# Transposing the layer's input on TensorE instead of loading it already transposed

## The chip, the cores and the metric

The kernel runs on one core of a Trainium2 chip. The metric is the device time of one execution in microseconds, the median of several runs. The profile shows one execution of it.

## The reference, cut to what matters

One decoder layer over 1024 tokens with 1024 features each, and 16 meta tokens ahead of them. The part that the change touches is the first product:

```python
h = jnp.concatenate([meta, x], axis=1)      # (1, 16 + 1024, 1024)
proj = h @ w_in                              # q, k, v, o_pre and 8 gate columns
...                                          # mLSTM mixer, @ w_out, layer norm
y = hier_moe(h, ...)                         # 32 experts, top 2, gated MLP
h = layer_norm(ALPHA * h + y, ...)
```

All products are computed in close to full float32: each operand is split into a rounded part and a remainder (`hi` and `lo`), and three matmuls (hi·hi, hi·lo, lo·hi) make one product.

## The kernel before, in words

The contraction of `h @ w_in` runs over the features, so TensorE needs the input with features on the partitions and tokens in the columns. The kernel before gets it so from memory: the host wrapper makes `x_cols`, the tokens reordered into 8 tiles of 128 features (partitions) by 8 chunks by 128 tokens, and `meta_cols`, the same for the meta tokens. It makes `x_rows` too, in the ordinary order, which is read later as the residual.

A tile of 512 KB is loaded by `load_x(n)` (L365) on SP's queue into one of two buffers `xt`. For each half tile ScalarE writes the rounded part `xhi` (`x_hi`, L670) and VectorE the remainder `xlo` (`x_lo`, L1011), both straight from `xt`. The weight comes in pieces of 512 columns. Of the first piece four quarters are loaded one by one (L370); ScalarE rounds them in eight steps of 512 elements (`hi_first`, L657) and VectorE subtracts in eight steps (`lo_first`, L999). Later pieces go in halves of 2048 elements (L648, L994).

TensorE does units in order. The first 8 (`o_unit(0)` to `o_unit(7)`) multiply token tile n by the first piece: 8 chunks of 3 matmuls, 24 matmuls of 128x512 (`mm3`, L1645 to L1647). Ahead of unit 0 it runs 14 dummy float32 matmuls on the identity (`awake`, L1723), after unit 7 the gate columns (`gate_rows`, L1680, L1682), then the units of the other pieces, then eight chunks of the mLSTM recurrence mixed with value and output products, the router, and the loop over the experts. Each engine does its list in the order in which it is written; what an engine waits for is a semaphore count that another engine's instruction raises (`x_hi`, `x_lo`, `hi_done`, `lo_done`).

`unit_cp` counts the evacuations of units by ScalarE (`evac`, L683). PSUM has eight banks; in the units banks 0 to 2 take the products, 3 to 7 the gate work, and bank 7 the dummy matmuls.

The mLSTM chunks use a selector `sel`, and two arrays `cm_rows` and `wi_rows` of which only 12 of the 128 partitions hold data; the others are zeroed by GpSimd at the start (L543, L544). `scores` multiplies `sel` by `cm_rows` (L1785) and `weight_rows` multiplies `sel` by `wi_rows` (L1804), both over all 128 partitions.

The same kernel transposes on TensorE elsewhere: `gated_T` (L1846), `z_T`, and in the expert loop `rows_T` (L1994), which transposes 128 gathered rows of 1024 features by 8 instructions of 128x128 into two PSUM banks; ScalarE (L826) and VectorE (L1489) then make `xghi` and `xglo` from the banks. `gate_tokens` (L1688) transposes nine blocks of 16 partitions.

Of the kernel before, what the change touches and what calls it, by code (L numbers as in the profile page):

```python
# [15 lines left out]
NMETA = 16
T = 1024
NT = T // P
NG = NT + 1
TA = T + NMETA  # L20
H = 4
# [29 lines left out]
def wait(eng, sem, value):  # L51

    if isinstance(value, int) and value <= 0:
        return
    eng.wait_ge(sem, value)


def tile_cols(m):

    return slice(NMETA + m * P, NMETA + (m + 1) * P)  # L60
# [6 lines left out]

def build(nc, x_rows, x_cols, meta_cols, w_in, b_gates, head_norm_w, w_out, ln1_g, ln1_b, w_group, b_group, w_router,
          b_router, w_gate, w_up, w_down, ln2_g, ln2_b, out):
# [13 lines left out]
    def at(name, shape, dt=F32):  # L83
        n = 1
        for s in shape[1:]:
            n *= s
        t = nc.alloc_sbuf_tensor_at(name, list(shape), dt, offset=cursor[0])
        offsets[name] = cursor[0]
        cursor[0] += (n * (2 if dt == BF16 else 4) + 31) // 32 * 32
        assert cursor[0] <= nc.sbuf_usable_end, (name, cursor[0])  # L90
        return t

    ident = at("ident", [P, P])
# [5 lines left out]
    ones = at("ones", [P, 4])  # L99
    sel = at("sel", [P, H, P], BF16)  # L100
    cm_rows = at("cm_rows", [P, NT, P], BF16)
    wi_rows = at("wi_rows", [P, NT, P], BF16)
    hnw = at("hnw", [P, KC])
# [46 lines left out]
    xhi = at("xhi", [P, KC, TA], F32R)  # L150
    xlo = at("xlo", [P, KC, TA], F32R)
# [5 lines left out]
    xt_at = cursor[0]  # L157
    xt = [at(f"xt{i}", [P, KC, P]) for i in range(2)]
    stage = [at(f"stage{i}", [P, 512]) for i in range(3)]
# [5 lines left out]
    cursor[0] = gate_at  # L165
    xtm = at("xtm", [P, KC, NMETA])
    cursor[0] = xt_at
# [29 lines left out]
    def over(t, name, shape, dt=F32):  # L197
        return nc.alloc_sbuf_tensor_at(name, list(shape), dt, offset=offsets[t])

    kTm = over("ks", "kTm", [P, H, 2 * NMETA])  # L200
    xhl = over("lg", "xhl", [P, KC, 2 * NMETA], F32R)
    hres = [over(f"qkT{i}", f"hres{i}", [P, D]) for i in range(2)]
# [76 lines left out]
    ps = [nc.alloc_psum_tensor(f"bank{i}", [P, 512], F32) for i in range(8)]  # L279
# [12 lines left out]
    def sem(name):  # L292
        if name not in S:
            S[name] = nc.alloc_semaphore(name)
        return S[name]

    first_landed = [sem(f"first_landed{s}") for s in range(4)]
# [5 lines left out]
    xt_landed = [sem(f"xt_landed{s}") for s in range(2)]  # L303
# [3 lines left out]
    res_landed = [sem(f"res_landed{s}") for s in range(2)]  # L307
# [6 lines left out]

    names = """wg_in small_in xm_landed ln1_in consts x_hi x_lo wg_hi wg_lo wo_hi wo_lo grow_mm grow_cp
        gtok_mm g_cols g_logs b_mm aT_mm m_rows mb_mm g_arg gate_exp
# [7 lines left out]
    N = {n: sem(n) for n in names}  # L324
# [9 lines left out]
    def unit(u):  # L334

        if u < Q0:
            return ("o", u // NT, u % NT)
        if u < K0:
            return ("q", (u - Q0) // H, (u - Q0) % H)
        return ("k", (u - K0) // H, (u - K0) % H)  # L340
# [6 lines left out]
    def lo_count(g):  # L347

        return KC + 2 * g

# [5 lines left out]
    def _(sp):  # L356
# [6 lines left out]
        def load_x(n):  # L363
            wait(sp, N["x_lo"], 2 * (n - 1))
            sp.dma_start(xt[n % 2][:], x_cols[n]).then_inc(xt_landed[n % 2], 16)  # L365

        load_x(0)
        for part in range(4):
            c = slice(part * 1024, (part + 1) * 1024)
# [4 lines left out]
        sp.dma_start(hnw[:], head_norm_w.rearrange("(p k) -> p k", k=KC)).then_inc(N["small_in"], 16)  # L374
        sp.dma_start(xtm[:], meta_cols).then_inc(N["xm_landed"], 16)
        load_x(2)
# [5 lines left out]

        sp.wait_ge(N["consts"], 2)
        sp.wait_ge(N["cm_split"], 1)
# [20 lines left out]
        def load_residual(i):  # L405
            if i < 2:
                sp.wait_ge(N["qs_done"], 7 + i)
                sp.wait_ge(N["kx_mm"], 8)
            else:
                sp.wait_ge(N["z_done"], 2 * (i - 1))  # L410
            sp.dma_start(hres[i % 2][:], x_rows[i * P:(i + 1) * P, :]).then_inc(res_landed[i % 2], 16)

# [103 lines left out]
        for q in range(2):  # L516
            sp.wait_ge(N["f_out"], NT + q)
            c = slice(q * 512, (q + 1) * 512)
# [6 lines left out]
    def _(pool):  # L525
        g = nc.gpsimd
# [15 lines left out]
        g.affine_select(out=selpos[:], in_=selpos[:], compare_op=ALU.not_equal, fill=1.0, base=0, pattern=[[-1, H], [0, P]], channel_multiplier=1)  # L542
        g.memset(cm_rows[:], 0.0)  # L543
        g.memset(wi_rows[:], 0.0)  # L544
        for i in range(3):
# [96 lines left out]
    def _(act):  # L642
        a = nc.scalar
# [9 lines left out]

        def hi_first(k):
            act.wait_ge(first_landed[k // 2], 16)
            c = slice(k * 512, (k + 1) * 512)
            a.activation(whi[0][:, c], raw[0][:, c], ACT.Copy).then_inc(N["hi_done"], 1)  # L657
# [8 lines left out]
        def x_hi(n):  # L666
            for q in (2 * n, 2 * n + 1):
                ks_ = slice(4 * (q % 2), 4 * (q % 2) + 4)
                act.wait_ge(xt_landed[n % 2], 16 * (n // 2 + 1))
                a.activation(xhi[:, ks_, tile_cols(n)], xt[n % 2][:, ks_, :], ACT.Copy).then_inc(N["x_hi"], 1)  # L670

        def x_hi_meta():
            act.wait_ge(N["xm_landed"], 16)
            a.activation(xhl[:, :, 0:NMETA], xtm[:], ACT.Copy)
            a.activation(xhi[:, :, 0:NMETA], xtm[:], ACT.Copy).then_inc(N["x_hi"], 1)

# [16 lines left out]
        x_hi(0)  # L693
        for k in range(KC):
            hi_first(k)
        x_hi(1)
# [258 lines left out]
    def _(dve):  # L955
        v = nc.vector
        tt, ts, stt = v.tensor_tensor, v.tensor_scalar, v.scalar_tensor_tensor
# [37 lines left out]

        def lo_first(k):
            dve.wait_ge(N["hi_done"], k + 1)
            c = slice(k * 512, (k + 1) * 512)
            tt(wlo[0][:, c], raw[0][:, c], whi[0][:, c].bitcast(F32), ALU.subtract).then_inc(N["lo_done"], 1)  # L999
# [7 lines left out]
        def x_lo(n):  # L1007
            for q in (2 * n, 2 * n + 1):
                ks_ = slice(4 * (q % 2), 4 * (q % 2) + 4)
                dve.wait_ge(N["x_hi"], q + 1)  # L1010
                tt(xlo[:, ks_, tile_cols(n)], xt[n % 2][:, ks_, :], xhi[:, ks_, tile_cols(n)].bitcast(F32), ALU.subtract).then_inc(N["x_lo"], 1)  # L1011

        x_lo(0)
        for k in range(KC):
            lo_first(k)
        x_lo(1)
# [6 lines left out]
        dve.wait_ge(N["x_hi"], 2 * NT + 1)  # L1023
        tt(xhl[:, :, NMETA:], xtm[:], xhi[:, :, 0:NMETA].bitcast(F32), ALU.subtract)
        v.tensor_copy(spread_rows[:].rearrange("r (a t) -> r a t", t=NMETA), ident[0:NMETA, 0:NMETA].unsqueeze(1).to_broadcast([NMETA, 2, NMETA]))
        tt(xlo[:, :, 0:NMETA], xtm[:], xhi[:, :, 0:NMETA].bitcast(F32), ALU.subtract).then_inc(N["x_lo"], 1)

# [612 lines left out]
    def _(pe):  # L1640
        t = nc.tensor

        def mm3(out, lh, ll, rh, rl, first, last):

            t.matmul(out, lh, rh, start=first, stop=False)  # L1645
            t.matmul(out, lh, rl, start=False, stop=False)  # L1646
            return t.matmul(out, ll, rh, start=False, stop=last)  # L1647

        def chunked(w):
            return w[:].rearrange("p (k n) -> p k n", k=KC)  # L1650

        def o_unit(u, ks_=range(KC)):
            _, piece, n = unit(u)
            wait(pe, N["unit_cp"], u - 2)
            wh, wl, c = chunked(whi[piece]), chunked(wlo[piece]), tile_cols(n)
            for k in ks_:
                if u == 0:
                    pe.wait_ge(N["lo_done"], k + 1)
                last = mm3(ps[u % 3][:], xhi[:, k, c], xlo[:, k, c], wh[:, k, :], wl[:, k, :], k == 0, k == KC - 1)
                if k == KC - 1:  # L1660
                    last.then_inc(N["unit_mm"], 1)
# [59 lines left out]
        def awake(bank, n):  # L1721
            for _ in range(n):
                t.matmul(ps[bank][:, 0:P], ident[:], ident[:], start=True, stop=True)  # L1723

        pe.wait_ge(N["consts"], 1)
        awake(7, 14)
        pe.wait_ge(N["x_lo"], 2)
        for u in range(NT):
            pe.wait_ge(N["x_lo"], 2 * u + 2)
            o_unit(u)  # L1730
        pe.wait_ge(N["consts"], 2)
        gate_rows()
# [181 lines left out]
        for c in range(NT):  # L1914
# [10 lines left out]
            half = [values, out_half][c == NT - 1]  # L1925
            args = [(5 + 2 * c,), (0, 1)][c == NT - 1]
# [176 lines left out]
        for n in range(EARLY):  # L2103
            last = t.matmul(ps[5][:, 2 * n:2 * n + 2], last_hot[:, n, :], last_cols[:, 2:4], start=True, stop=True)
# [41 lines left out]
```

## Time and profile before

| | |
|---|---|
| median of 3 runs | 1124.6 us (1123.21 to 1126.51) |
| the profiled execution | 1124.6 us, of which its span is 1122.8 us |
| TensorE busy | 1093.7 us, 97% of the span |
| VectorE / ScalarE / GpSimd busy | 799.9 / 626.4 / 216.0 us |

The times of the profile count from the start of the span. TensorE is the engine to look at first; the first 60 us hold all that the change touches in the kernel's order, apart from the small matmuls on `sel`.

### The profile page before, as it was taken

What the parts mean: (1) busy time and instruction counts of PE and PEld (TensorE: products, weight loads), DVE (VectorE), ACT (ScalarE), POOL (GpSimd) and SP (SyncE); (2) the same over time, 40 slices, a digit from 0 to 9 for tenths busy, and PEclk for the clock granted to TensorE, in tenths of its full rate; (3) what the DMA queues carried; (4) which work ended last, traced back from release to release, by engine and by line L of the source; (5) the groups of instructions that cost most, each with busy time, mean ns of one, the idle gap of its engine ahead of it and who ended that gap; (6) DMA issues with size and microseconds to landing.
All of it is one profiled execution on the core that took longest, in us unless ns stands there. A gap on an engine that the chain in (4) does not pass through costs nothing.

```text
span 1122.8 us, 15319 instructions
## 1 busy us (share of the span) xinstructions
PE 1093.7 (97%) x5369; PEld 899.2 (80%) x5369; DVE 799.9 (71%) x1127; ACT 626.4 (56%) x698; POOL 216.0 (19%) x188
## 2 busy tenths in 40 slices
PE   8999999999999999979999999999999999999986
PEld 7778899788888787858888888888888888888852
DVE  4220422144557787679999999998989989898787
ACT  5312222224335310147887878778788888888644
POOL 4000112000000000020434323143332423323110
PEclk9999999999999999999999999999999999999998
DMA  8612314802123222159999999999999999999885
GB/s 304 224 50 101 122 43 129 276 20 75 39 77 114 113 76 94 54 203 381 398 380 367 397 375 390 391 380 394 378 380 383 385 389 370 391 392 379 312 328 217
DMA packets 69273, 288.32 MB, mean 257 GB/s; under 512 B 16229, under 2 KB 20453, under 8 KB 43620
## 3 DMA queue, kind: packets, MB, share of 16 engines
q1 hardware_dynamic: 56224, 258.34, 60.7%
q0 software_dynamic: 11840, 25.09, 6.1%
q10 hardware_dynamic: 1156, 4.20, 1.0%
q8 instruction: 32, 0.52, 0.2%
q14 instruction: 21, 0.17, 0.0%
HBM read 266.66 MB, written 37.75 MB: 271 GB/s over the span
## 4 chain that ended last, share of the span: by engine, by line
PE 93%; DVE 3%; DMA 2%; issue 1%; ACT 0%; DVEq 0%; POOL 0%; POOLq 0%; ACTq 0%
PE bank L1645 26%; PE bank L1647 26%; PE bank L1646 26%; PE bank L1994 3%; PE bank L2094 1%; PE bank L2029 1%; PE bank L1832 1%; PE bank L1834 1%; PE bank L1881 1%; PE bank L1837 1%; DMA expert_rows<-yt,dix 1%; PE bank L1846 1%; PE bank L1790 1%; PE bank L1873 1%; DMA xg<-h_rows,tokrow 1%
## 5 line engine op out<-in xcount | busy, mean ns | idle before, releaser
L1645 PE MATMUL bank<-whi,xghi 128*128 128x512 f32 x512 | 203.5, 397 | 0.6 <-DVE xglo L1489 0.6
L1647 PE MATMUL bank<-whi,xglo 128*128 128x512 f32 x512 | 200.6, 392 | 0.0
L1646 PE MATMUL bank<-wlo,xghi 128*128 128x512 f32 x512 | 200.2, 391 | 0.0
L1476 DVE TENSOR_TENSOR wlo<-raw_down,whi 128x2048 fp32r<-128x2048 f32 x64 | 146.3, 2291 | 28.0 <-ACT whi L819 27.9
L1645 PE MATMUL bank<-whi,xhi 128*128 128x512 f32 x384 | 156.2, 407 | 0.9 <-ACT num L762 0.6
L1647 PE MATMUL bank<-whi,xlo 128*128 128x512 f32 x384 | 151.7, 395 | 0.0
L1646 PE MATMUL bank<-wlo,xhi 128*128 128x512 f32 x384 | 151.7, 395 | 0.0
L1476 DVE TENSOR_TENSOR wlo<-raw,whi 128x2048 fp32r<-128x2048 f32 x64 | 146.3, 2288 | 4.5 <-ACT whi L819 3.6
L1476 DVE TENSOR_TENSOR wlo<-raw_up,whi 128x2048 fp32r<-128x2048 f32 x64 | 146.2, 2285 | 0.0
L819 ACT ACTIVATE whi<-raw_up 128x2048 fp32r<-128x2048 f32 x64 | 122.4, 1915 | 25.8 <-PE bank L1647 25.4
L819 ACT ACTIVATE whi<-raw_down 128x2048 fp32r<-128x2048 f32 x64 | 122.4, 1912 | 23.7 <-PE bank L1647 23.7
L609 POOL DMA_INDIRECT expert_rows<-yt,dix x32 | 60.7, 1898 | 377.2 <-ACT yt L842 365.1
L819 ACT ACTIVATE whi<-raw 128x2048 fp32r<-128x2048 f32 x64 | 122.4, 1914 | 9.9 <-DVE h1t L1210 4.6
L1647 PEld LDWEIGHTS bank<-whi,xglo 128*128 128x128 f32 x512 | 96.7, 189 | 20.8
L1645 PEld LDWEIGHTS bank<-whi,xghi 128*128 128x128 f32 x512 | 97.1, 190 | 20.1 <-DVE xglo L1489 1.0
L1646 PEld LDWEIGHTS bank<-wlo,xghi 128*128 128x128 f32 x512 | 96.8, 189 | 19.2
L1645 PE MATMUL bank<-whi,ghi 128*128 128x512 f32 x256 | 102.2, 399 | 0.3 <-DVE glo L1498 0.3
L1647 PE MATMUL bank<-whi,glo 128*128 128x512 f32 x256 | 100.2, 391 | 0.0
L1646 PE MATMUL bank<-wlo,ghi 128*128 128x512 f32 x256 | 100.1, 391 | 0.0
L599 POOL DMA_INDIRECT xg<-h_rows,tokrow x16 | 30.1, 1879 | 309.4 <-DMA h_rows<-z 293.8
L1647 PEld LDWEIGHTS bank<-whi,xlo 128*128 128x128 f32 x384 | 72.5, 189 | 17.4
L1645 PEld LDWEIGHTS bank<-whi,xhi 128*128 128x128 f32 x384 | 72.8, 190 | 16.9 <-issue 1.8
(342 smaller groups left out, 1715.7 us busy)
## 6 DMA issues: line engine op xcount, KB each, us to landing
raw<-l_w_gate SPq DMA_DIRECT2D x64, 1024.0 KB, 8.3
raw_up<-l_w_up SPq DMA_DIRECT2D x64, 1024.0 KB, 8.4
raw_down<-l_w_down SPq DMA_DIRECT2D x64, 1024.0 KB, 8.6
raw<-l_w_in SPq DMA_DIRECT2D x5, 2048.0 KB, 10.0
yy<-expert_rows SPq DMA_DIRECT2D x8, 1024.0 KB, 7.9
xt<-x_cols SPq DMA_DIRECT2D x8, 512.0 KB, 4.9
o_rows<-stage POOLq DMA_DIRECT2D x16, 256.0 KB, 2.9
qkT<-qk_rows SPq DMA_DIRECT2D x16, 256.0 KB, 3.8
```

The source lines that it names most:

```text
L599: g.indirect_dma_start(xg[b][:], None, h1_dram[0:T, :], bass.IndirectOffsetOnAxis(rows.bitcast(U32), 0), bounds_check=last_token, oob_is_e ...
L609: g.indirect_dma_start(ys[0:rows, :], bass.IndirectOffsetOnAxis(dix[b][:].bitcast(U32), 0), yt[b][:], None, bounds_check=last_row if bound ...
L819: a.activation(whi[k][:, halves(p)], raw_e[k][:, halves(p)], ACT.Copy).then_inc(e_hi[k], 1)
L1476: tt(wlo[k][:, halves(p)], raw_e[k][:, halves(p)], whi[k][:, halves(p)].bitcast(F32), ALU.subtract).then_inc(e_lo[k], 1)
L1645: t.matmul(out, lh, rh, start=first, stop=False)
L1646: t.matmul(out, lh, rl, start=False, stop=False)
L1647: return t.matmul(out, ll, rh, start=False, stop=last)
L1790: last = t.matmul(ps[F_BANK[1]][:, h * P:(h + 1) * P], qkT[b][:, 1, h, :], qkT[b][:, 0, h, :], start=True, stop=True)
L1832: t.matmul(ps[N_BANK[h % 2]][:, 0:DV + 1], ew[:, h, :], vext[c % 2][:, h, :], start=True, stop=False)
L1834: t.matmul(ps[N_BANK[h % 2]][:, 0:DV + 1], qsT[:, h, :], cst[:, h, :], start=False, stop=True).then_inc(N["n_mm"], 1)
L1837: t.matmul(ps[U_BANK[h % 2]][:, 0:DV + 1], ks[:, h, :], vext[c % 2][:, h, :], start=True, stop=True).then_inc(N["u_mm"], 1)
L1994: last = t.transpose(ps[q][:, k * P:(k + 1) * P], xv[:, 4 * q + k, :], ident[:])
```

## The change

The host wrapper no longer makes the transposed copies. One array `hcat` holds the meta tokens and then the tokens as rows; `load_x(n)` loads 128 rows of 4 KB from it, the residual loads read it too, and `xtm` is now 16 rows of 4 KB.

`x_T(n)` on TensorE transposes a tile by 8 instructions into two of the banks 4 to 7, and `x_T_meta` the meta tokens by 8 small ones into bank 4. `x_hi` and `x_lo` read the banks. SP's load of tile n waits for the transposes of tile n-2 (`xT_mm`) and not for their `x_lo`. On TensorE `x_T(0)` stands after the second dummy matmul, with nine more after it (11 in all, before 14); `x_T(1)` stands inside unit 0 after chunk 5, `x_T(2)` behind unit 0, `x_T(3)` to `x_T(7)` behind units 1 to 5, and `x_T_meta` behind unit 6. The first piece is split in four steps of 1024 elements. `sel`, `cm_rows` and `wi_rows` shrink to 12 partitions, and their zeroing in GpSimd's list goes.

```diff
-    sel = at("sel", [P, H, P], BF16)
-    cm_rows = at("cm_rows", [P, NT, P], BF16)
-    wi_rows = at("wi_rows", [P, NT, P], BF16)
+    sel = at("sel", [3 * H, H, P], BF16)
+    cm_rows = at("cm_rows", [3 * H, NT, P], BF16)
+    wi_rows = at("wi_rows", [3 * H, NT, P], BF16)
...
-    xt = [at(f"xt{i}", [P, KC, P]) for i in range(2)]
+    xt = [at(f"xt{i}", [P, D]) for i in range(2)]
-    xtm = at("xtm", [P, KC, NMETA])
+    xtm = at("xtm", [NMETA, D])
...
         def load_x(n):
-            wait(sp, N["x_lo"], 2 * (n - 1))
-            sp.dma_start(xt[n % 2][:], x_cols[n]).then_inc(xt_landed[n % 2], 16)
+            wait(sp, N["xT_mm"], 2 * (n - 1))
+            sp.dma_start(xt[n % 2][:], hcat[tile_cols(n), :]).then_inc(xt_landed[n % 2], 16)
...
-        sp.dma_start(xtm[:], meta_cols).then_inc(N["xm_landed"], 16)
+        sp.dma_start(xtm[:], hcat[0:NMETA, :]).then_inc(N["xm_landed"], 16)
...
-        sp.wait_ge(N["consts"], 2)
         sp.wait_ge(N["cm_split"], 1)
...
-            sp.dma_start(hres[i % 2][:], x_rows[i * P:(i + 1) * P, :])...
+            sp.dma_start(hres[i % 2][:], hcat[tile_cols(i), :])...
...
-        g.memset(cm_rows[:], 0.0)
-        g.memset(wi_rows[:], 0.0)
...
-        def hi_first(k):
-            act.wait_ge(first_landed[k // 2], 16)
-            c = slice(k * 512, (k + 1) * 512)
+        def hi_first(part):
+            act.wait_ge(first_landed[part], 16)
+            c = slice(part * 1024, (part + 1) * 1024)
...
-                act.wait_ge(xt_landed[n % 2], 16 * (n // 2 + 1))
-                a.activation(xhi[:, ks_, tile_cols(n)], xt[n % 2][:, ks_, :], ACT.Copy).then_inc(N["x_hi"], 1)
+                act.wait_ge(N["xT_mm"], q + 1)
+                a.activation(xhi[:, 4 * half:4 * half + 4, tile_cols(n)], ps[4 + q % 4][:]..., ACT.Copy).then_inc(N["x_hi"], 1)
...
-                tt(xlo[:, ks_, tile_cols(n)], xt[n % 2][:, ks_, :], xhi[...], ALU.subtract).then_inc(N["x_lo"], 1)
+                tt(xlo[cols], ps[4 + q % 4][:]..., xhi[cols].bitcast(F32), ALU.subtract).then_inc(N["x_lo"], 1)
...
+        def x_T(n):
+            pe.wait_ge(xt_landed[n % 2], 16 * (n // 2 + 1))
+            xv = xt[n % 2][:].rearrange("p (m k) -> p k m", k=KC)
+            for half in range(2):
+                q = 2 * n + half
+                wait(pe, N["x_lo"], q - 3)
+                for k in range(4):
+                    last = t.transpose(ps[4 + q % 4][:, k * P:(k + 1) * P], xv[:, 4 * half + k, :], ident[:])
+                last.then_inc(N["xT_mm"], 1)
+
+        def x_T_meta():
+            pe.wait_ge(N["xm_landed"], 16)
+            xv = xtm[:].rearrange("p (m k) -> p k m", k=KC)
+            pe.wait_ge(N["x_lo"], 2 * NT - 3)
+            for k in range(KC):
+                last = t.transpose(ps[4][:, k * NMETA:(k + 1) * NMETA], xv[:, k, :], ident[0:NMETA, 0:NMETA])
+            last.then_inc(N["xT_mm"], 1)
...
-                if u == 0:
-                    pe.wait_ge(N["lo_done"], k + 1)
+                if u == 0 and k % 2 == 0:
+                    pe.wait_ge(N["lo_done"], k // 2 + 1)
...
-        awake(7, 14)
+        awake(7, 2)
+        x_T(0)
+        awake(7, 9)
         pe.wait_ge(N["x_lo"], 2)
-        for u in range(NT):
+        o_unit(0, range(0, 6))
+        x_T(1)
+        o_unit(0, range(6, KC))
+        x_T(2)
+        for u in range(1, NT):
             pe.wait_ge(N["x_lo"], 2 * u + 2)
             o_unit(u)
+            if u + 2 < NT:
+                x_T(u + 2)
+            if u == NT - 2:
+                x_T_meta()
...
-    tokens = np.ascontiguousarray(x[0])
-    by_column = tokens.reshape(NT, P, P, KC).transpose(0, 2, 3, 1)
-    meta_by_column = np.asarray(meta_tokens).reshape(NMETA, P, KC).transpose(1, 2, 0)
+    rows = np.concatenate([np.asarray(meta_tokens), x[0]])
+    arrays = {"hcat": rows}
```

## Rows read from the trace of the kernel before

**Rows 1.** The page, part 1: the first engine's busy time in the span.

```profile
PE 1093.7 (97%) x5369; PEld 899.2 (80%) x5369; DVE 799.9 (71%) x1127; ACT 626.4 (56%) x698; POOL 216.0 (19%) x188
```

**Rows 2.** The page, part 4: shares of the chain that ended last.

```profile
PE 93%; DVE 3%; DMA 2%; issue 1%; ACT 0%; DVEq 0%; POOL 0%; POOLq 0%; ACTq 0%
```

**Rows 3.** Windows, busy us of each engine, granted clock, DMA share, GB/s.

```profile
core 0: us, PE busy (x) PEld busy (x) DVE busy (x) ACT busy (x) POOL busy (x), PEclk, DMA share, GB/s
30.00:53.00 23.00, 23.00 (x101) 18.63 (x100) 7.56 (x9) 8.48 (x12) 2.17 (x4) 1.00 0.69 249
...
505.00:1060.00 555.00, 555.00 (x2641) 464.93 (x2641) 509.17 (x342) 446.58 (x372) 169.91 (x109) 1.00 0.98 380
```

**Rows 4.** Timeline of the opening: start us, us, instruction, idle before it.

```profile
3.28 5.52 PE L1723 MATMUL bank<-ident 128*128 128x128 f32 x28 [3.28 <-POOL ident L537]
...
4.17 1.15 ACT L670 ACTIVATE xhi<-xt 128x512 fp32r<-128x512 f32 x2 [2.08 <-DMA xt<-x_cols]
...
4.83 1.29 DVE L1011 TENSOR_TENSOR xlo<-xt,xhi 128x512 fp32r<-128x512 f32 x2 [4.83 <-ACT xhi L670]
...
5.59 1.15 ACT L657 ACTIVATE whi<-raw 128x512 fp32r<-128x512 f32 x2 [0.27 <-DMA raw<-l_w_in]
...
6.25 1.97 DVE L999 TENSOR_TENSOR wlo<-raw,whi 128x512 fp32r<-128x512 f32 x2
...
7.88 1.15 ACT L657 ACTIVATE whi<-raw 128x512 fp32r<-128x512 f32 x2 [1.15 <-DMA raw<-l_w_in]
...
8.55 4.26 DVE L999 TENSOR_TENSOR wlo<-raw,whi 128x512 fp32r<-128x512 f32 x6 [0.33 <-ACT whi L657]
...
8.55 0.48 PE L1645 MATMUL bank<-whi,xhi 128*128 128x512 f32 x1
...
9.20 1.15 ACT L657 ACTIVATE whi<-raw 128x512 fp32r<-128x512 f32 x2 [0.17 <-DMA raw<-l_w_in]
...
12.15 1.15 ACT L670 ACTIVATE xhi<-xt 128x512 fp32r<-128x512 f32 x2 [0.31 <-DMA xt<-x_cols]
...
14.19 0.47 PE L1645 MATMUL bank<-whi,xhi 128*128 128x512 f32 x1
...
14.27 1.15 ACT L670 ACTIVATE xhi<-xt 128x512 fp32r<-128x512 f32 x2 [0.81 <-DMA xt<-x_cols]
...
20.97 1.15 ACT L670 ACTIVATE xhi<-xt 128x512 fp32r<-128x512 f32 x2 [3.64 <-DMA xt<-x_cols]
```

**Rows 5.** The chain that ended last, one `rows_T`: start us, us, what.

```profile
578.33 0.89 PE bank L1994 x8
```

**Rows 6.** Timeline at the first `rows_T`, which meets TensorE at rest.

```profile
502.39 1.76 PE L1994 MATMUL bank<-ident,xg 128*128 128x128 f32 x8 [3.13 <-DMA xg<-h_rows,tokrow]
...
503.33 0.60 ACT L826 ACTIVATE xghi<-bank 128x512 fp32r<-128x512 f32 x1 [5.97 <-PE bank L1994]
503.96 0.69 DVE L1489 TENSOR_TENSOR xglo<-bank,xghi 128x512 fp32r<-128x512 f32 x1 [2.77 <-ACT xghi L826]
504.18 0.60 ACT L826 ACTIVATE xghi<-bank 128x512 fp32r<-128x512 f32 x1 [0.26 <-PE bank L1994]
```

**Rows 7.** Instruction groups by shape: busy us, mean ns of one.

```profile
L994 DVE TENSOR_TENSOR wlo<-raw,whi 128x2048 fp32r<-128x2048 f32 x2 | 4.5, 2289 | 1.0 <-ACT whi L648 1.0
L648 ACT ACTIVATE whi<-raw 128x2048 fp32r<-128x2048 f32 x2 | 3.7, 1902 | 0.0
```

**Rows 8.** The chain that ended last, the transposes of `gate_tokens`.

```profile
66.46 0.66 PE bank L1688 x9
```

**Rows 9.** Instruction groups by shape, weight loads of 32 and of 128 partitions.

```profile
L1832 PEld LDWEIGHTS bank<-vext,ew 128*128 128x128 f32 x64 | 12.2, 190 | 2.0
...
L1820 PEld LDWEIGHTS bank<-vext,ks 32*128 32x128 f32 x8 | 1.3, 184 | 1.1 <-DVE cst L1113 0.6 <-issue 0.4
```

**Rows 10.** Windows, columns as in rows 3: a stretch at a lower granted clock.

```profile
226.00:230.00 4.00, 4.00 (x11) 3.14 (x12) 1.09 (x4) 0.00 (x0) 0.00 (x0) 0.57 0.02 0
```

More of the change, by code:

```diff
@@ L65, in halves, with build @@
     return slice(p * HALF, (p + 1) * HALF)
-def build(nc, x_rows, x_cols, meta_cols, w_in, b_gates, head_norm_w, w_out, ln1_g, ln1_b, w_group, b_group, w_router,
+def build(nc, hcat, w_in, b_gates, head_norm_w, w_out, ln1_g, ln1_b, w_group, b_group, w_router,
           b_router, w_gate, w_up, w_down, ln2_g, ln2_b, out):
@@ L313, in build @@
     rows_landed = [sem(f"rows_landed{n}") for n in range(NT)]
-    names = """wg_in small_in xm_landed ln1_in consts x_hi x_lo wg_hi wg_lo wo_hi wo_lo grow_mm grow_cp
+    names = """wg_in small_in xm_landed ln1_in consts xT_mm x_hi x_lo wg_hi wg_lo wo_hi wo_lo grow_mm grow_cp
         gtok_mm g_cols g_logs b_mm aT_mm m_rows mb_mm g_arg gate_exp
@@ L347, in lo_count @@
     def lo_count(g):
-        return KC + 2 * g
+        return 4 + 2 * g
     def units_stored(s, u):
@@ L410, in load_residual @@
                 sp.wait_ge(N["z_done"], 2 * (i - 1))
-            sp.dma_start(hres[i % 2][:], x_rows[i * P:(i + 1) * P, :]).then_inc(res_landed[i % 2], 16)
+            sp.dma_start(hres[i % 2][:], hcat[tile_cols(i), :]).then_inc(res_landed[i % 2], 16)
         def load_expert(j, e, k, parts=range(2)):
@@ L667, in x_hi @@
             for q in (2 * n, 2 * n + 1):
-                ks_ = slice(4 * (q % 2), 4 * (q % 2) + 4)
-                act.wait_ge(xt_landed[n % 2], 16 * (n // 2 + 1))
-                a.activation(xhi[:, ks_, tile_cols(n)], xt[n % 2][:, ks_, :], ACT.Copy).then_inc(N["x_hi"], 1)
+                half = q % 2
+                act.wait_ge(N["xT_mm"], q + 1)
+                a.activation(xhi[:, 4 * half:4 * half + 4, tile_cols(n)], ps[4 + q % 4][:].rearrange("p (k t) -> p k t", k=4), ACT.Copy).then_inc(N["x_hi"], 1)
         def x_hi_meta():
-            act.wait_ge(N["xm_landed"], 16)
-            a.activation(xhl[:, :, 0:NMETA], xtm[:], ACT.Copy)
-            a.activation(xhi[:, :, 0:NMETA], xtm[:], ACT.Copy).then_inc(N["x_hi"], 1)
+            act.wait_ge(N["xT_mm"], 2 * NT + 1)
+            a.activation(xhl[:, :, 0:NMETA], ps[4][:, 0:KC * NMETA].rearrange("p (k t) -> p k t", k=KC), ACT.Copy)
+            a.activation(xhi[:, :, 0:NMETA], ps[4][:, 0:KC * NMETA].rearrange("p (k t) -> p k t", k=KC), ACT.Copy).then_inc(N["x_hi"], 1)
         def evac(u):
@@ L693, in _ @@
         x_hi(0)
-        for k in range(KC):
-            hi_first(k)
+        for part in range(4):
+            hi_first(part)
         x_hi(1)
@@ L994, in lo, with lo_first @@
                 tt(wlo[g % 2][:, c], raw[g % 2][:, c], whi[g % 2][:, c].bitcast(F32), ALU.subtract).then_inc(N["lo_done"], 1)
-        def lo_first(k):
-            dve.wait_ge(N["hi_done"], k + 1)
-            c = slice(k * 512, (k + 1) * 512)
+        def lo_first(part):
+            dve.wait_ge(N["hi_done"], part + 1)
+            c = slice(part * 1024, (part + 1) * 1024)
             tt(wlo[0][:, c], raw[0][:, c], whi[0][:, c].bitcast(F32), ALU.subtract).then_inc(N["lo_done"], 1)
@@ L1008, in x_lo @@
             for q in (2 * n, 2 * n + 1):
-                ks_ = slice(4 * (q % 2), 4 * (q % 2) + 4)
+                half = q % 2
                 dve.wait_ge(N["x_hi"], q + 1)
-                tt(xlo[:, ks_, tile_cols(n)], xt[n % 2][:, ks_, :], xhi[:, ks_, tile_cols(n)].bitcast(F32), ALU.subtract).then_inc(N["x_lo"], 1)
+                cols = (slice(None), slice(4 * half, 4 * half + 4), tile_cols(n))
+                tt(xlo[cols], ps[4 + q % 4][:].rearrange("p (k t) -> p k t", k=4), xhi[cols].bitcast(F32), ALU.subtract).then_inc(N["x_lo"], 1)
         x_lo(0)
-        for k in range(KC):
-            lo_first(k)
+        for part in range(4):
+            lo_first(part)
         x_lo(1)
@@ L1023, in _ @@
         dve.wait_ge(N["x_hi"], 2 * NT + 1)
-        tt(xhl[:, :, NMETA:], xtm[:], xhi[:, :, 0:NMETA].bitcast(F32), ALU.subtract)
+        tt(xhl[:, :, NMETA:], ps[4][:, 0:KC * NMETA].rearrange("p (k t) -> p k t", k=KC), xhi[:, :, 0:NMETA].bitcast(F32), ALU.subtract)
         v.tensor_copy(spread_rows[:].rearrange("r (a t) -> r a t", t=NMETA), ident[0:NMETA, 0:NMETA].unsqueeze(1).to_broadcast([NMETA, 2, NMETA]))
-        tt(xlo[:, :, 0:NMETA], xtm[:], xhi[:, :, 0:NMETA].bitcast(F32), ALU.subtract).then_inc(N["x_lo"], 1)
+        tt(xlo[:, :, 0:NMETA], ps[4][:, 0:KC * NMETA].rearrange("p (k t) -> p k t", k=KC), xhi[:, :, 0:NMETA].bitcast(F32), ALU.subtract).then_inc(N["x_lo"], 1)
         dve.wait_ge(N["grow_mm"], 1)
@@ L2132 @@
     x = np.asarray(x)
-    tokens = np.ascontiguousarray(x[0])
-    by_column = tokens.reshape(NT, P, P, KC).transpose(0, 2, 3, 1)
-    meta_by_column = np.asarray(meta_tokens).reshape(NMETA, P, KC).transpose(1, 2, 0)
-    arrays = {"x_rows": tokens, "x_cols": np.ascontiguousarray(by_column), "meta_cols": np.ascontiguousarray(meta_by_column)}
-    args = [nc.dram_tensor(name, a.shape, F32, kind="ExternalInput").ap() for name, a in arrays.items()]
+    rows = np.concatenate([np.asarray(meta_tokens), x[0]])
+    arrays = {"hcat": rows}
+    args = [nc.dram_tensor("hcat", rows.shape, F32, kind="ExternalInput").ap()]
     for name in _INS:
```

## The prediction

> **What bounds the kernel now.** I read the page's first part first, for the engine that is nearly always busy. TensorE is busy for 97% of the span [rows 1]. The chain of work that ended last says whether this matters, since a busy engine can still wait at the places that count: 93% of the chain is TensorE, 3% VectorE, 2% DMA [rows 2]. Then the windows, because the change sits in the first 55 us and a mean over the span says nothing of them. In 30 to 53 us TensorE is busy for 23.00 of 23.00 us at a granted clock of 1.00, and the same holds for the expert loop (555 of 555 us) [rows 3]. So in the units that the change enlarges TensorE has no hole into which a new instruction could fall. VectorE (7.6 of 23 us) and ScalarE (8.5 of 23 us) have room there.
>
> Last the timeline of the opening, instruction by instruction, because there the work depends on loads. The dummy matmuls run from 3.28 us until the first real one at 8.55. Unit 1 begins at 14.19, 5.64 us later, for 24 matmuls and so 0.235 us each; the later units keep that pace. The tiles of x land just before ScalarE takes them: 0 at 4.15, 1 at 12.15, 2 at 14.27, 3 at 20.97. Of the weight quarters the first is there by 5.59, the second by 7.88, the third by 9.20 [rows 4].
>
> **The change, part by part.**
>
> *Transposes between the units.* TensorE gets 8 tiles of 8 transposes, 64 instructions that it did not do before. The expert loop does exactly this form (128 rows of 1024 float32, read with a stride of 8 elements, the identity as the other operand): 8 transposes hold the chain for 0.89 us [rows 5], 0.11 us each. Tiles 1 to 7 stand in a stream without holes: 7 x 0.89 = 6.23 us. Tile 0 stands among the dummy matmuls and is costed below.
>
> *Meta transposes.* 8 instructions of 16 partitions behind unit 6. The nearest row is `gate_tokens`, nine transposes of 16 partitions in 0.66 us [rows 8]: 8 x 0.073 = 0.59 us. Both load 16 partitions of 128 columns, so I take it unchanged; at the full price of a tile it would be 0.89.
>
> *The opening.* Here the order is x lands, transpose, ScalarE, VectorE, then the first weight quarter, then TensorE. The nearest stretch is the first `rows_T`: it too follows a rest, and its 8 transposes take 1.76 us instead of 0.89 [rows 6]. The dummy matmuls at 3.28 are slow in the same way: 28 records in 5.27 us are 0.19 each, between the 0.11 and 0.22 that a transposed block takes in rows 5 and 6. If they run at 0.22 first and 0.11 then, 28 records fit when the faster pace comes after 4.4 us, at about 7.7. So:
>
> - two dummies (4 records, 0.88 us) end about when tile 0 lands, 4.15; `x_T(0)` runs 4.15 to 5.9;
> - ScalarE starts its first half 0.94 us after the transposes begin and its second at 1.79, VectorE its first at 1.57 [rows 6]: `xhi` ends at 6.55, `xlo` at 7.2. Before, ScalarE was done with tile 0 at 5.3 [rows 4];
> - a quarter of 1024 elements costs ScalarE between half of 1.90 and the 1.15 of two steps of 512, I take 1.0; VectorE between half of 2.29 and 1.42 (a third of 4.26 for six steps of 512), I take 1.2 [rows 4, 7]. First quarter: ScalarE 6.55 to 7.55, VectorE 7.6 to 8.8;
> - nine dummies are 18 records from 5.9: 8 until 7.7 at 0.22, ten more at 0.11, end 8.8.
>
> Unit 0 then begins at about 8.9 instead of 8.55: +0.35. The first quarter sets that, and the dummies would set nearly the same. If VectorE is slowed as in its first pair before (1.97 us for two steps, beside GpSimd's work) [rows 4], the start is 9.6; if all is quick, it is 8.55. The bounds of this term are 0 and +1.05.
>
> *Coarser steps.* TensorE must now wait for a whole quarter. Second quarter: ScalarE 7.9 to 8.9, VectorE until 10.1, wanted at 8.9 + 1.5 = 10.4. Third: landed 9.20, ScalarE 10.2, VectorE 11.4, wanted at 11.8. `x_T(1)` follows at 13.2, tile 1 landed at 12.15, so no wait. The fourth is done while it runs. `x_T(2)` at 15.6 meets a tile that landed at 14.27, and unit 1 at 16.5 finds `xlo` of tile 1 some time ready (transposed by 14.1, then 0.6 + 0.7 us twice over at most). Cost zero, hidden by TensorE's own stream; without that cover each late quarter would cost the difference, 0.3 us in the second's case if the start is early.
>
> *The waits on loads.* `x_T(n)` blocks TensorE's queue, where before only `x_lo` waited; behind it stand all later units. Tile 3 landed at 20.97, and its load now leaves SP when `x_T(1)` is done, 14.1, practically when it left before, behind a 2 MB weight piece. `x_T(3)` stands behind unit 1, at 22.1: 1.1 us of cover. The later tiles leave on `x_T(n-2)`, some 6 us after one another as TensorE takes them, and have more. If tile 3 were later by 2 us, it would cost 0.9. I take 0. A tile is 512 KB in rows of 4 KB per partition before and after; the meta load and the residual loads move the same bytes.
>
> *PSUM instead of SBUF as source.* ScalarE's half tile is 0.60 us from a bank and 0.58 (half of 1.15) from `xt`; VectorE's 0.69 from a bank and 0.65 from `xt` [rows 4, 6]. Both engines have room [rows 3]. The waits of a transpose for `x_lo` four halves earlier are long met. Zero.
>
> *Twelve partitions.* 64 small matmuls on `sel` (four in `scores` and four in `weight_rows` for each of 8 chunks) read 12 partitions instead of 128. A weight load of 32 partitions takes 184 ns, of 128 partitions 190 [rows 9], so the height of an operand buys nothing. The two memsets stood behind the identity in GpSimd's list and nobody on the path waits for them. The removed wait for `consts` on SP comes after four weight pieces and was long met. Zero; the bounds are 0 and a gain of their whole stream time. That is an estimate: 128 columns are a quarter of the 512 that take 0.235 us, so 0.059 each and 3.8 us for 64; rows 9 make it remote.
>
> Sum: 6.23 + 0.59 + 0.35 = 7.17 us. Everything behind unit 7 starts from TensorE's end, so nothing gives it back: the stalls later (VectorE 3% of the chain) hang on TensorE's own products. The profiled execution took 1124.6 us with a span of 1122.8, and 1124.6 is the median too: 1124.6 + 7.2 = 1131.8 us, 0.64% more. A difference of 0.3%, 3.4 us, is about what can be told from none.
>
> *The clock.* Transposes could count less than matmuls for the granted clock. In the expert loop 12 transposes stand to every 72 matmuls and the clock stays at 1.00 over 555 us [rows 3]; the units will have 8 to every 24, a denser mix that no row shows. The Trainium skill, "TensorE: Matmul & The Clock Gate", section "Part 4: PE-mode transpose", says that transpose mode does not engage the full clock, as it does not count as PE-busy in the same way. By the trace the sum is 7.2; by that rule it would be more, as the first rival has it. The trace speaks against it only for the thinner mix.
>
> **The rivals.**
>
> *A. The clock falls in the units, or rises later.* The stretch 226 to 230 us ran at a mean of 0.57 [rows 10]: four microseconds in which 0.43 x 4 = 1.7 us of full-clock work was lost. One such stretch more is +1.7, so 1133.5; one behind each of `x_T(2)` to `x_T(7)` is +10.3, so 1142. In the opening, if the 1.76 us of `x_T(0)` count as rest, the faster pace comes 1.8 us later, nine dummies end at 9.8 and not 8.8: +0.9, so 1132.7. For it: the denser mix. Against: rows 3. Chance 0.07 for a form that leaves the range below, 0.13 for a small one.
>
> *B. Transposes are hidden or the total is within 0.3%.* The dip at 226 to 230 follows a stretch of small matmuls and might not come again once all is shifted: -1.7, so 1130.1. If the twelve-row matmuls also took no time, the 3.8 us above would come off: 1126.3, no difference. Against: rows 9, and TensorE without a hole in rows 3. Chance 0.05.
>
> *C. Faster than before, by lighter small matmuls.* The place is `scores` and `weight_rows` in the eight chunks. Their own time is worth 3.8 us at most. To turn the sign it must bring more than 7.2, to be seen as faster 10.6: three times their own time, so each chunk would have to lose 1.3 us because ScalarE and VectorE, which wait for these banks, begin sooner. Against: rows 9, and the 93% of the chain that lies on TensorE itself [rows 2]. Chance 0.02.
>
> *D. A wait takes the place.* TensorE blocks on a tile, for instance tile 3 by 2 us late (+0.9) or tile 4 and 5 too, as their loads now hang on TensorE's order: +1 to +3, so 1133 to 1135. For it: each load has only two buffers. Against: the margins above. Chance 0.10.
>
> **How the numbers follow.** The forecast, plain addition of TensorE's time, has 0.63; the rest is A (0.07 + 0.13), B 0.05, C 0.02, D 0.10. The range takes in the small form of A and all of D upward, and downward the lost dip with the fast opening (1131.8 - 1.7 - 0.35 = 1129.7), with the runs' own spread of 1.4 us below the median: 1128.5 to 1135. Left out are the large form of A, B's equality and C, 0.14. Slower by over 0.3% (above 1128.0) takes everything but B's equality and C: 0.93; within 0.3% 0.05; faster 0.02.
>
> **What would show it.** In the profile after, unit 1 should begin at about 16.4 us, later units every 6.5 us instead of 5.6 (24 x 0.235), and the first matmul of `gate_rows` some 7.2 us later than before. `x_T` should appear as eight groups of 8 at 0.11 us, only the first at 0.22. The expert loop should begin 7 us later and last as long. The idle time ahead of the transposes should be zero; if it names a DMA, D holds. A granted clock under 1.00 before 60 us is A. An equal time with the transposes present would mean that the sum is right in the opening and given back, which I would look for in 215 to 380 us, where the 12-row matmuls are.

## The result, and the profile after

The changed kernel takes 1138.35 us (median of 4 runs, 1136.37 to 1139.71) against 1123.9 us before, a ratio of 1.0125 (95% interval 1.0104 to 1.0144): 14 us slower. A second comparison, taken later with the mended forms beside it, gave 1.0124 (1.0108 to 1.0140). The direction was forecast; the size was twice the forecast 7.2 us, and the time lies above the range.

The page of the changed kernel, parts 1 and 4, answers to [rows 1, 2]:

```profile
PE 1109.4 (98%) x5435; PEld 909.1 (80%) x5435; DVE 798.8 (70%) x1123; ACT 625.1 (55%) x694; POOL 211.7 (19%) x186
...
PE 93%; DVE 3%; DMA 2%; issue 1%; ACT 1%; DVEq 0%; POOL 0%; POOLq 0%; ACTq 0%
```

TensorE is busy for 15.7 us longer, and the chain is still TensorE's. So nearly all of the loss is TensorE's own time, but the sum said 7.2. To see where, take the same instruction in both traces and subtract the starts. The timeline of TensorE in the changed kernel, opening and units:

```profile
3.28 1.23 PE L1739 MATMUL bank<-ident 128*128 128x128 f32 x4 [3.28 <-POOL ident L536]
4.30 1.96 PE L1657 MATMUL bank<-ident,xt 128*128 128x128 f32 x8
6.06 2.59 PE L1739 MATMUL bank<-ident 128*128 128x128 f32 x18
9.36 0.47 PE L1643 MATMUL bank<-whi,xhi 128*128 128x512 f32 x1 [0.71 <-DVE wlo L996]
...
22.37 1.05 PE L1657 MATMUL bank<-ident,xt 128*128 128x128 f32 x8
...
28.83 1.05 PE L1657 MATMUL bank<-ident,xt 128*128 128x128 f32 x8
...
54.44 0.39 PE L1645 MATMUL bank<-whi,xlo 128*128 128x512 f32 x1
54.75 1.05 PE L1665 MATMUL bank<-ident,xtm 16*128 16x16 f32 x8
55.73 0.50 PE L1643 MATMUL bank<-whi,xhi 128*128 128x512 f32 x1
...
61.40 0.34 PE L1696 MATMUL bank<-xhi,wg 128*16 128x400 f32 x1
```

This part went nearly as summed. From `x_T(3)` at 22.37 to `x_T(4)` at 28.83 is 6.46 us (forecast 6.5), with no wait on a load ahead of either. The gate columns begin at 61.40; before they began at 53.19: the units and transposes have cost 8.2 us, against 7.17 in the sum.

The lag then stays at 8.2 us until the recurrence and grows there. On the chain, the last `h_rows<-z` store before the experts starts at 491.25 before and at 507.21 after, 15.96 us later. Up to the eighth chunk every chunk adds about 1.1 us: the `scores` of the eight chunks start 8.2, 9.3, 10.4, 11.6, 12.6, 13.7, 14.8 and 15.9 us later than before, so seven chunks carry the loss. The eighth adds nothing. There TensorE waited 0.64 us for VectorE before (366.63, the row below) and does not wait after, so the time that `scores` takes longer falls into that wait. Two lines of the timeline and two of the chain, first before, then after:

```profile
366.63 0.40 PE L1804 MATMUL bank<-wi_rows,sel 128*128 128x128 bf16 x4 [0.64 <-DVE ew L1118]
491.25 3.73 DMA h_rows<-z
...
382.72 0.39 PE L1830 MATMUL bank<-wi_rows,sel 12*128 12x128 bf16 x4
507.21 2.75 DMA h_rows<-z
```

The timeline shows where the 1.1 us are. `scores` in the changed kernel, with weight loads (PEld) and matmuls (PE):

```profile
227.42 0.10 PEld L1810 LDWEIGHTS bank<-maskb,identb 128*128 128x128 bf16 x1 [0.36 <-issue]
227.43 0.23 PE L1810 MATMUL bank<-maskb,identb 128*128 128x128 bf16 x1
227.59 0.09 PEld L1811 LDWEIGHTS bank<-cm_rows,sel 12*128 12x128 bf16 x1
227.59 0.22 PE L1811 MATMUL bank<-cm_rows,sel 12*128 12x128 bf16 x1
...
227.74 0.10 PEld L1810 LDWEIGHTS bank<-maskb,identb 128*128 128x128 bf16 x1
227.75 0.23 PE L1810 MATMUL bank<-maskb,identb 128*128 128x128 bf16 x1
...
228.54 0.22 PE L1811 MATMUL bank<-cm_rows,sel 12*128 12x128 bf16 x1
...
228.70 1.16 PE L1816 MATMUL bank<-qkT 128*128 128x128 f32 x8
```

The same place in the kernel before:

```profile
219.23 0.23 PE L1784 MATMUL bank<-maskb,identb 128*128 128x128 bf16 x1
219.24 0.10 PEld L1785 LDWEIGHTS bank<-cm_rows,sel 128*128 128x128 bf16 x1
219.29 0.22 PE L1785 MATMUL bank<-cm_rows,sel 128*128 128x128 bf16 x1
...
219.68 1.11 PE L1790 MATMUL bank<-qkT 128*128 128x128 f32 x8
```

The durations (second column) tell nothing: a matmul lasts 0.22 to 0.23 us in both. The starts (first column) do. Before, the weight load of the next matmul begins 0.01 us after the running one, and matmuls start 0.056 us apart. After, load and matmul of `sel` both begin only 0.16 us behind the running one. The eight matmuls take 1.27 us (227.43 to 228.70) instead of 0.45 (219.23 to 219.68). They are the ones that now alternate between 128 and 12 partitions. The other 0.2 to 0.3 us of a chunk lie around `weight_rows`, four matmuls of 12 partitions in a row between higher ones: it and the work up to the next transposes take 3.75 us instead of 3.50. The forecast had costed that edit at zero.

Behind the recurrence some of the lag comes back: from the start of the `h_rows<-z` store to the landing of the first gather on the chain it is 8.9 us in this trace, 11.0 before. At the first `rows_T` of the expert loop the lag is 13.86 us, from the second one to the last it is 13.04.

### The profile page after: what moved, and what is told of

It is laid out like the page before. It is cut to its first block, busy times and chain, and to the rows that moved or that the text cites. A ratio compares the mean times of both kernels' runs of the same rounds, so it can differ in the third digit from the quotient of the medians.

```text
span 1136.3 us, 15447 instructions
## 1 busy us (share of the span) xinstructions
PE 1109.4 (98%) x5435; PEld 909.1 (80%) x5435; DVE 798.8 (70%) x1123; ACT 625.1 (55%) x694; POOL 211.7 (19%) x186
## 4 chain that ended last, share of the span: by engine, by line
PE 93%; DVE 3%; DMA 2%; issue 1%; ACT 1%; DVEq 0%; POOL 0%; POOLq 0%; ACTq 0%
PE bank L1643 26%; PE bank L1645 25%; PE bank L1644 25%; PE bank L2020 2%; PE bank L2120 1%; PE bank L2055 1%; PE bank L1858 1%; PE bank L1860 1%; PE bank L1863 1%; PE bank L1907 1%; DMA expert_rows<-yt,dix 1%; PE bank L1657 1%; PE bank L1816 1%; PE bank L1872 1%; PE bank L1899 1%
```

## The experiments

Three questions: does the height of the three arrays carry the loss in the recurrence; what is the rule; and what do the transposes cost by themselves. In what follows "lag" is the start of an instruction less its start in the first trace of the kernel before. One execution is traced in each run, so the changed kernel has two traces (its own and after_again), every other kernel one. Times are medians; a difference in us with an interval is the ratio's, times 1124 us.

**after_128_rows.** Undo one part: the changed kernel with the arrays at full height.

```diff
-    sel = at("sel", [3 * H, H, P], BF16)
-    cm_rows = at("cm_rows", [3 * H, NT, P], BF16)
-    wi_rows = at("wi_rows", [3 * H, NT, P], BF16)
+    sel = at("sel", [P, H, P], BF16)
+    cm_rows = at("cm_rows", [P, NT, P], BF16)
+    wi_rows = at("wi_rows", [P, NT, P], BF16)
...
+        sp.wait_ge(N["consts"], 2)
...
+        g.memset(cm_rows[:], 0.0)
+        g.memset(wi_rows[:], 0.0)
```

> The changed kernel with sel, cm_rows and wi_rows back at 128 partitions and their zeroing back; the transposes stay. Theory, height change: in the changed kernel's trace the matmuls of scores step by 0.155 us instead of 0.056 wherever one of 128 partitions and one of 12 follow each other, and the recurrence lost 7.7 us; with 128 partitions the lag behind the kernel before stays at the 8.2 us that it has when the first 8 units end, so 1124 + 8.2 = 1132 us. Rival, shift: the recurrence loses because everything is later or because of the clock, whatever the operands' height: 1138 us, and steps of 0.155 us are gone but the lag grows all the same.

1128.88 us, ratio to before 1.0039 (1.0026 to 1.0052), and 9.5 us under the changed kernel's first median. `scores` takes 0.46 us again:

```profile
227.66 0.23 PE L1813 MATMUL bank<-maskb,identb 128*128 128x128 bf16 x1
227.73 0.22 PE L1814 MATMUL bank<-cm_rows,sel 128*128 128x128 bf16 x1
...
228.12 0.55 PE L1819 MATMUL bank<-qkT 128*128 128x128 f32 x3
```

The lag is 8.46 us at the gate columns and 8.53 at the store (499.78), and 8.50 at the eighth `scores`. So the recurrence loses nothing when the height is back, and the shift theory falls. The time is lower than the expected 1132; that is taken up below.

**before_12_rows.** Do that part alone: the kernel before, with the arrays at 12 partitions and their zeroing gone.

> The kernel before with the three arrays at 12 partitions and without their zeroing, no transposes. Height change: no lag until 219 us, then 1.1 us in each of seven chunks, 7.7 in all, so up to 1131.7 us, less what differs in how fast the gathers before the expert loop land (2.9 us in the two traces so far). Rival, shift: 1124 us.

1130.86 us, ratio 1.0061 (1.0049 to 1.0074). `scores` takes 1.27 us; the lag grows by 1.1 us a chunk, from -0.39 at the gate columns to 5.7 at the store. That is 6.1. The trace of before has the stretch at a low granted clock of [rows 10] in its first chunk (22.60 us from one `scores` to the next), this trace does not have it; before_delay_8, also without it, takes 21.04. So 1.6 us more of the loss are hidden by the comparison: 7.7, as expected. The part that was costed at nothing costs 6 to 7 us by itself (difference of the medians 6.0, ratio times 1124 us 6.9).

**before_12_rows_grouped.** Is a low matmul slow, or is the change between heights? Same arrays, other order.

```diff
             for h in range(H):
-                out_h = ps[F_BANK[0]][:, h * P:(h + 1) * P]
-                t.matmul(out_h, identb[:], maskb[:], start=True, stop=False)
-                last = t.matmul(out_h, sel[:, h, :], cm_rows[:, c, :], start=False, stop=True)
+                t.matmul(ps[F_BANK[0]][:, h * P:(h + 1) * P], identb[:], maskb[:], start=h == 0, stop=False)
+            for h in range(H):
+                last = t.matmul(ps[F_BANK[0]][:, h * P:(h + 1) * P], sel[:, h, :], cm_rows[:, c, :], start=False, stop=h == H - 1)
```

> As before_12_rows, but scores issues its four mask matmuls of 128 partitions first and then its four of 12: eight changes of height per chunk in scores become two. Height change: 6 x 0.10 us saved in each of 7 chunks, 4.2 us less than before_12_rows, about 1127.5. Rival, slow matmul: a matmul of 12 partitions itself takes 0.2 us longer in a stream, whatever stands beside it: same time as before_12_rows, 1131.7.

1128.02 us, ratio 1.0029 (1.0018 to 1.0041); 2.8 us under before_12_rows. The timeline of the second chunk:

```profile
243.07 0.39 PE L1781 MATMUL bank<-maskb,identb 128*128 128x128 bf16 x4
243.39 0.39 PE L1783 MATMUL bank<-cm_rows,sel 12*128 12x128 bf16 x4
```

Four low matmuls in a row take 0.39 us, exactly as four high ones do. `scores` is now 0.64 to 0.65 us long: 0.19 more than before for two changes of height, where eight cost 0.82. So a change costs 0.10 us and the low matmul itself nothing. The lag grew by 3.3 us over the recurrence where 7.7 less 4.2 were expected, 3.5. The time fell by less than 4.2 us, but the intervals of the two ratios allow 4.2, so the prices of single changes rest on the traces and not on the times.

**before_100_rows.** The rule: does any height below 128 count?

> The kernel before with the three arrays at 100 partitions, zeroed as before. Theory, strips: what counts is into how many strips of rows the array is split for a matmul, and 100 partitions need the undivided array as 128 do: 1124 us and steps of 0.056 us. Rival, any height other than 128 counts as a change: 1131.7 us, steps of 0.155.

1124.32 us, ratio 1.0003 (0.9992 to 1.0015): no difference. The second chunk:

```profile
240.29 0.22 PE L1784 MATMUL bank<-maskb,identb 128*128 128x128 bf16 x1
240.35 0.22 PE L1785 MATMUL bank<-cm_rows,sel 100*128 100x128 bf16 x1
...
240.76 0.66 PE L1790 MATMUL bank<-qkT 128*128 128x128 f32 x4
```

**before_64_rows.**

> The kernel before with the three arrays at 64 partitions, zeroed. Theory, strips: 100 partitions behaved as 128 and 12 did not, so a half array of 64 should count as another division: steps of 0.155 us in scores and about the time of before_12_rows, 1130.9 (6.0 more than before). Rival, only a quarter array (up to 32 partitions) has to be changed to: steps of 0.056 us and the time of before.

1132.33 us, ratio 1.0082 (1.0069 to 1.0095):

```profile
219.21 0.23 PE L1784 MATMUL bank<-maskb,identb 128*128 128x128 bf16 x1
219.38 0.23 PE L1785 MATMUL bank<-cm_rows,sel 64*128 64x128 bf16 x1
...
220.49 0.71 PE L1790 MATMUL bank<-qkT 128*128 128x128 f32 x4
```

1.28 us for the eight, like 12 partitions. The border lies above 64 and at or below 100. This kernel keeps the zeroing by GpSimd, as before_100_rows does, so the missing memsets of before_12_rows are not what costs. In the trace the recurrence loses as much as with 12 partitions (6.1 us, and the 1.6 that the comparison hides). The time was 9.3 us over before where 6.0 were expected, a miss upward; its interval (7.8 to 10.7 us) overlaps that of before_12_rows (5.5 to 8.3), and whether 64 partitions cost more than 12 is not shown. The Trainium skill, "TensorEngine Tiling (Array Packing)", section "Key Properties", says that changing the tiling mode drains TensorE. The Trainium skill, on the same page, section "Available Configurations", lists modes of 128, 64 and 32 rows. The traces fit this: 100 partitions as 128, 12 and 64 apart from them, 0.10 us at each change. A drain itself no trace shows.

**after_100_rows.** The mended form of the changed kernel, and **after_again** beside it on the same chip.

> The changed kernel with the three arrays at 100 partitions, zeroed. Strips: as after_128_rows, 4 to 6 us over before, and steps of 0.056 us in scores; the lag that unit 7 leaves (8.2 to 8.5 us) does not grow in the recurrence. Rival, shift: it stays with the changed kernel.

> The changed kernel once more, beside its mended forms on one chip. 14.4 us slower than before in the first comparison; the two parts alone gave 4.0 (transposes, after_128_rows) and 6.0 (12 partitions, before_12_rows), together 10.0. If the parts simply add, a second comparison comes nearer to 10 to 12 us; if they make each other worse, it stays at 14.

after_100_rows takes 1130.61 us, ratio 1.0054 (1.0040 to 1.0067); after_again 1137.71 us, 1.0124 (1.0108 to 1.0140). The lag of after_100_rows is 8.12 us at the gate columns and 8.03 at the store. (Its trace lacks the low-clock stretch of the first chunk and has one near 443 us instead, which comes to about the same; at the eighth `scores` the lag is 6.7.) More than half of what the change lost is gone with one number, and 12 partitions cost 7.1 us on top of the transposes. The parts: 4.4 and 6.1 us for the transposes in two comparisons (0.39% and 0.54% of 1124), 6.9 for the height, 11 to 13 together; the whole is 13.9 with an interval of 12.1 to 15.7. Within the intervals they add.

**before_delay_8 and before_delay_16.** The transposes made TensorE 8.5 us late and the time only 4.4 to 6.1 us longer. Here the kernel before is only made late, by 38 dummies ahead of the gate columns, or 72 in before_delay_16.

```diff
+        awake(7, 38)
         pe.wait_ge(N["consts"], 2)
         gate_rows()
```

> The kernel before with 38 more dummy matmuls (0.222 us each, 8.4 us) between unit 7 and the gate columns, nothing else. The trace of after_128_rows lay 8.5 us behind until 480 us, but its timed runs were only 4.0 us slower. Theory, given back by lateness: what the later stages lose (low granted clock at 226 to 230 and 502 to 510 us, landing of the gathers) depends on when they come, so a bare delay of 8.4 us costs about 4 us as well. Rival, plain addition: 8.4 us, and then the transposes themselves have brought something back elsewhere.

> The same with 72 dummies, 16.0 us, as late as the changed kernel is at 480 us. By lateness the time should be near that of the changed kernel, 14.4 us more than before; by plain addition 16.0. If 8.4 us cost 4 and 16 cost 14, the loss of the changed kernel is more than that of its two parts because of where the stages fall.

1130.36 us, ratio 1.0058 (1.0046 to 1.0071), for a lag of 8.48; 1138.02 us, 1.0138 (1.0121 to 1.0155), for one of 16.30. In us that is 6.5 (5.2 to 8.0) and 15.5 (13.6 to 17.4). The first shows that a bare delay of that length is not paid in full: 8.5 lies outside its interval. The second, where 14.4 or 16.0 were expected, can't be told from either nor from full price. The size that I expected for the first, 4 us, was not met, though the intervals of it and of after_128_rows (2.9 to 5.8) overlap. Two places of the chain, here in before_delay_8, show what can come back:

```profile
499.63 3.13 DMA h_rows<-z
503.59 5.55 DMA xg<-h_rows,tokrow
```

Before, these two were 3.73 and 6.43 us. In all eight traces of kernels with transposes or a delay the store took 2.75 to 3.13 us; in the five without (before, 100, 64, 12 and 12 grouped) 3.57 to 3.76. The gather took 5.26 to 5.59 in seven of the eight and 6.28 to 6.49 in four of the five; the exceptions are after_128_no_meta with 6.81 and before_100_rows with 5.35. So from the start of the store to the landing of the gather before_delay_8 is 1.5 us quicker than before. Lateness at the store does not explain it: after_128_no_meta starts the store at 497.00 us and takes 2.98, before_12_rows and before_64_rows start it at 496.96 and 497.29 and take 3.76 and 3.71. What the eight quick ones share is that they are 7 us or more late already at the gate columns. The other place is the granted clock: the first trace of before had it low for 3.4 us around 226 to 230 [rows 10] and for 7 us around 502 to 510, the traced before_delay_8 for some 3 us near 444 and again near 503. Both also have it low for some microseconds after 1090. Where it falls differs between two executions of one kernel too: the first trace of the changed kernel has it low from about 234 to 239 us, after_again does not, and the first chunk takes 23.74 us in one and 22.18 in the other.

For before_delay_8 the steps can be read one by one. The lag is 8.5 us at the first chunk and 6.9 at the second, as its trace lacks the stretch at 226. It is 8.4 at the store, after the stretch at 444, and 6.9 when the gather has landed. In the expert loop it is 4.5, because its stretch near 503 falls on dummy matmuls, and the one of before falls on the first products. At the last matmul it is 5.9. So 1.5 us come back by the store and the gather and the rest by where the low-clock stretches fell in these two executions. How much a single trace can differ shows before_100_rows: it is 3.8 us ahead of the first trace of before in the expert loop, though the medians agree. What sets the store's time or the clock's stretches was not found.

**after_128_no_meta.** What do the meta transposes cost? They are left out and the meta tokens loaded transposed, as before; the three arrays have 128 partitions.

```diff
-        sp.dma_start(xtm[:], hcat[0:NMETA, :]).then_inc(N["xm_landed"], 16)
+        sp.dma_start(xtm[:], meta_cols).then_inc(N["xm_landed"], 16)
...
-            if u == NT - 2:
-                x_T_meta()
```

> after_128_rows with the meta tokens loaded already transposed, as in the kernel before, and x_T_meta left out. In the changed kernel's trace the 8 meta transposes hold TensorE for 1.06 us, from 54.67 to 55.73, where I had summed 0.59. Height change: they are 16 partitions high, so they pay for going to another division and back besides 8 x 0.12 us; without them the lag after unit 7 is 8.5 - 1.1 = 7.4 us. Rival: they hide something, and the lag stays over 8.

The lag at the gate columns is 7.2 us, 1.3 less than in after_128_rows. Of that 0.2 is the opening (unit 0 starts at 9.43 us, there at 9.65), so the meta transposes take 1.1, as their rows in the changed kernel say. The time, 1129.97 us, ratio 1.0050 (1.0034 to 1.0067), can't show 1 us.

**after_128_fine_first.** The changed kernel at 128 partitions, with the first weight piece in eight steps again.

> after_128_rows with the first weight piece split in eight steps of 512 again. In the changed kernel TensorE waits 0.71 us for the first step of 1024 and starts unit 0 at 9.36. With steps of 512, ScalarE's first is over at 7.4, VectorE's at about 8.3, before the dummies end at 8.65: unit 0 starts at 8.7 and the lag after unit 7 is 0.6 us less, about 7.8. Rival: the start is set by something else (the dummies' slow pace), and it stays at 9.3.

Unit 0 starts at 9.67 us, not at 8.7; the lag at the gate columns is 8.52. The timeline:

```profile
3.27 1.22 PE L1742 MATMUL bank<-ident 128*128 128x128 f32 x4 [3.27 <-POOL ident L537]
4.63 1.97 PE L1660 MATMUL bank<-ident,xt 128*128 128x128 f32 x8
6.39 3.52 PE L1742 MATMUL bank<-ident 128*128 128x128 f32 x18
9.67 0.48 PE L1646 MATMUL bank<-whi,xhi 128*128 128x512 f32 x1
```

Tile 0 landed 0.33 us later in this execution, and the 18 dummy records, 2.6 us long in the changed kernel, took 3.5: their pace doubled only shortly before their end. Here the dummies set the start, as the rival had it. They do so too in after_128_rows, which has the coarse steps and starts unit 0 at 9.65 us, and in after_again and after_100_rows (9.37 and 9.23), all without idle time ahead of it. So the coarse steps are not shown to cost anything. In the first trace of the changed kernel the coarse step did set the start, by its 0.71 us of idle time, and in after_128_no_meta by 0.63. Which of them ends last differs between executions of the same kernel. The one timed run, 1132.15 us, settles nothing about the time.

## Why the prediction was wrong

The step that failed is "Twelve partitions", costed at zero with the reason that "the height of an operand buys nothing" [rows 9] and with bounds of zero and a gain. Rows 9 show how long a weight load takes, and that was right: a load of 12 partitions takes 90 ns, of 128 partitions 98. What the edit changed was the distance between two matmuls of different heights, which no duration of one instruction shows. The runs put it at 0.10 us a change, eight in each `scores` and two around `weight_rows`, 1.1 us a chunk in seven chunks: 7.7 us of TensorE's time, measured as 6.9 us alone and 7.1 on top of the transposes. No bound looked at a loss, and no rival did: B and C asked only what lighter matmuls could save. The kernel before had a sign of it: `gate_tokens` starts 0.32 us after the matmul ahead of it (66.07 to 66.39), where the products stand 0.23 apart; its transposes are 16 partitions high.

The other points:

- *Transposes between the units*, 7 x 0.89 = 6.23 us: right, 0.89 a tile by the starts of `x_T(3)` and `x_T(4)` (6.46 less 24 x 0.232).
- *Meta transposes*, 0.59: mis-sized, 1.06 (54.67, one product's 0.23 after 54.44, to 55.73), 1.1 by leaving them out. They stand 0.11 us apart (8 in 1.05 us, the last of them 0.26 long) where those of `gate_tokens` stand about 0.07 apart, so the nearest row was not near enough. They are 16 partitions high, and the change of height ahead of them, 0.09 in the case of `gate_tokens`, was not in the row that I took. Why the steps differ is not shown.
- *The opening*, +0.35: +0.81 (9.36 instead of 8.55), inside its bounds of 0 and 1.05. In six traces of kernels with transposes it is +0.68 to +1.12, two of them above the bound. The order of events was right; ScalarE began 1.14 us after the transposes and not 0.94. In four of the six the dummies end last, as they take up their faster pace later than summed: that is the small form of rival A for the opening. The granted clock reads 1.00 over 5 to 10 us in all of them, so it does not show this change of pace.
- *Coarser steps, waits on loads, PSUM as source*: zero, as costed. No later transpose waits for a load, so rival D did not happen.
- *The clock*, rival A, its form for the units: there it stayed at 1.00 with 8 transposes to every 24 matmuls, as this window of the changed kernel shows. The rule of the Trainium skill on transposes ("TensorE: Matmul & The Clock Gate", "Part 4: PE-mode transpose") did not cost anything in this mix.

```profile
30.00:53.00 23.00, 23.00 (x113) 19.19 (x112) 9.56 (x10) 9.37 (x14) 2.16 (x4) 1.00 0.55 187
```

- *"Nothing gives it back"*: only partly. TensorE's 8.5 us of transposes were measured as 4.4 and 6.1 us, and a bare delay of 8.5 us as 6.5. Had the height been left alone, 7.2 us would have been above both medians, though inside the interval of one (4.5 to 7.5); the errors of the height and of this point had opposite signs. Why the store and the gather before the experts are quicker in the kernels with transposes stays open.

No version here beats the kernel before. The best with rows loaded untransposed is the changed kernel at 128 or 100 partitions, 0.4 to 0.5% slower than before.

## What to carry to other kernels

Count the changes of operand height in TensorE's stream, not only its instructions: here matmuls of 12 and of 64 partitions between matmuls of 128 cost 0.10 us at each change, where TensorE has no wait to hide it in. So pad small operands with zeros to the height of their neighbours (100 was enough here) or issue them together. When an edit looks free because each instruction lasts as long as before, look at the distance between starts. And bound every unknown on both sides, even where the edit only takes work away.

## What was not expected of the hardware

A matmul of 12 or 64 partitions next to one of 128 starts 0.158 us after it (eight in 1.27 and 1.28 us) instead of 0.056, and the weight load that otherwise runs ahead begins only with it; 100 partitions behave nearly as 128 (0.058). The last `h_rows` store before the experts takes 2.75 to 3.13 us in the eight traces that are late already at the gate columns and 3.57 to 3.76 in the five others, also where these reach the store as late as one of the eight; why was not found. And of two executions of the changed kernel one has a low granted clock from 234 to 239 us and the other has none there.
